# A two-layer hybrid trunk on one core: the LRU input joins the split products, and seven engine orders change

## What is computed

```python
h = rms_norm(x, norm_g)
proj = jnp.einsum('bsd,de->bse', h, w_in)
u_lru, u_s5, qkv_ret, q_nsa, kv_nsa, bg_nsa, gate_paths, merge = split_columns(proj, IN_SIZES)
...
ys = ys * jax.nn.silu(gate_paths.reshape(bsz, s, N_BRANCH, BRANCH_W))
branch = jnp.einsum('bsnw,nwd->bsnd', ys, w_branch)
merged = jnp.sum(jax.nn.sigmoid(merge.reshape(bsz, s, N_BRANCH, d)) * branch, axis=2)
return x + jnp.einsum('bsd,de->bse', merged, w_out)
```

## Time and profile before

| | |
|---|---|
| median of 3 runs | 856.46 us (855.59 to 857.69) |
| the profiled execution | 856.7 us, its span 854.9 us |
| TensorE matmuls busy | 796.3 us (93%) |
| VectorE, ScalarE, GpSimd busy | 517.6 (61%), 450.9 (53%), 305.2 us (36%) |
| mean granted TensorE clock | 0.961 |
| DMA | 126.6 MB, 148 GB/s over the span |

### The profile page before, as it was taken

How to read it: one execution, slowest core, us unless ns; L and a number is a source line. 1 busy time by engine, 2 the same in 40 slices (tenths; PEclk the granted TensorE clock), 3 DMA queues, 4 the chain that set the end, 5 groups by cost and what they waited for, 6 DMA issues and landing times.

```text
span 854.9 us, 11525 instructions
## 1 busy us (share of the span) xinstructions
PE 796.3 (93%) x4446; PEld 680.7 (80%) x4446; DVE 517.6 (61%) x761; ACT 450.9 (53%) x781; POOL 305.2 (36%) x135
## 2 busy tenths in 40 slices
PE   8786999899989899999989979998998989999996
PEld 8675889688978688887878868986897868888885
DVE  2957394477698551534686575547868875435335
ACT  5555786345752356553447297654474534545542
POOL 3000000005468576657400000000256775655860
PEclk9977999999998799999999989999999998999999
DMA  8518355466245434345435663535635344345541
GB/s 250 140 50 289 99 176 178 138 191 193 88 117 169 134 118 153 102 150 171 145 78 140 196 216 94 204 123 165 211 121 156 114 137 127 126 129 170 173 148 49
DMA packets 86998, 126.64 MB, mean 148 GB/s; under 512 B 22072, under 2 KB 32672, under 8 KB 86944
## 3 DMA queue, kind: packets, MB, share of 16 engines
q1 hardware_dynamic: 86768, 125.88, 47.5%
q10 hardware_dynamic: 176, 0.04, 0.0%
HBM read 124.85 MB, written 1.05 MB: 147 GB/s over the span
## 4 chain that ended last, share of the span: by engine, by line
PE 73%; ACT 9%; DVE 8%; issue 5%; POOL 2%; DMA 2%; ACTq 0%; POOLq 0%; DVEq 0%
PE proj L1662 52%; PE proj L1701 5%; PE M L1657 3%; ACT sc L698 2%; DMA raw<-in_w_in 2%; POOL w_lo L676 2%; PE M L1823 2%; ACT nkT L698 1%; ACT qT L698 1%; PE M L1976 1%; PE M L1981 1%; DVE sc L1539 1%; PE M L559 1%; ACT w_hi L698 1%; PE M L1824 1%
## 5 line engine op out<-in xcount | busy, mean ns | idle before, releaser
L676 POOL TENSOR_TENSOR w_lo<-raw,w_hi 128x1024 fp32r<-128x1024 f32 x112 | 287.1, 2596 | 501.2 <-ACT w_hi L698 469.9
L698 ACT ACTIVATE w_hi<-raw 128x1024 fp32r<-128x1024 f32 x192 | 197.4, 1055 | 125.0 <-DMA raw<-in_w_in 68.1
L1662 PE MATMUL proj<-w_hi,h_hi 128*128 128x512 f32 x544 | 220.5, 405 | 8.2 <-DVE w_lo L1247 7.7
L1662 PE MATMUL proj<-w_lo,h_hi 128*128 128x512 f32 x544 | 215.6, 396 | 0.0
L1662 PE MATMUL proj<-w_hi,h_lo 128*128 128x512 f32 x544 | 215.2, 396 | 0.0
L1662 PEld LDWEIGHTS proj<-w_hi,h_hi 128*128 128x128 f32 x544 | 104.3, 192 | 31.7 <-DVE w_lo L1247 8.5
L1662 PEld LDWEIGHTS proj<-w_hi,h_lo 128*128 128x128 f32 x544 | 104.2, 192 | 22.8
L1662 PEld LDWEIGHTS proj<-w_lo,h_hi 128*128 128x128 f32 x544 | 104.4, 192 | 21.0 <-issue 0.5
L1247 DVE TENSOR_TENSOR w_lo<-raw,w_hi 128x1024 fp32r<-128x1024 f32 x80 | 94.8, 1221 | 38.5 <-ACT w_hi L698 27.1
L1701 PE MATMUL proj<-h_full,raw 128*128 128x256 f32 x256 | 59.3, 393 | 7.8 <-ACT u_s L698 7.8
L1701 PEld LDWEIGHTS proj<-h_full,raw 128*128 128x128 f32 x256 | 50.1, 198 | 15.5 <-ACT u_s L698 8.3
(11 more groups left out here) (330 smaller groups left out, 1294.0 us busy)
## 6 DMA issues: line engine op xcount, KB each, us to landing
raw<-in_w_in SPq DMA_DIRECT2D x152, 512.0 KB, 3.7
raw<-in_w_branch SPq DMA_DIRECT2D x32, 512.0 KB, 3.6
raw<-in_w_out SPq DMA_DIRECT2D x16, 512.0 KB, 3.6
raw<-in_s_w_glu SPq DMA_DIRECT2D x8, 512.0 KB, 4.5
raw<-in_w_in SPq DMA_DIRECT2D x8, 256.0 KB, 2.6
merged<-in_nsa_ck_w SPq DMA_DIRECT2D x4, 512.0 KB, 5.2
mt<-in_nsa_ck_w SPq DMA_DIRECT2D x4, 512.0 KB, 6.8
merged<-in_nsa_cv_w SPq DMA_DIRECT2D x4, 512.0 KB, 4.6
```

Of the source, the lines that this page charges most:

```text
L676: nc.gpsimd.tensor_tensor(w_lo[:, slot(s, l), 0:n * w], raw[:, u % N_RAW, 0:n * w], w_hi[:, slot(s, l), 0:n * w].bitcast(f32), ALU.subtrac ...
L698: i = nc.scalar.activation(out_, in_, func, **kw)
L1662: last = mm(dst, left[i], right[j], start=start and n == 0, stop=stop and n == 2, skip_group_check=True)
```

## The change

u_lru leaves `NATIVE` and joins `LO_ON_VECTOR`: its four units are cast by ScalarE, their w_lo made by VectorE, and the chunk becomes a split product. Seven engine orders change with it:

1. ScalarE, start of a layer: the copy of u_s5 comes first, `keep_u` reads that copy, `keep_v0` stands before `trig(0)`, `spread_v(0)` behind the copies of cmp, and single casts stand between the copies up to ret_v. `spread_w(0)` now stands behind the wait for u_s5.
2. VectorE, start: `parameters_c` (cut off `parameters_b`) opens the layer; the h_lo stand before `make_w(1)`; the w_lo of u_lru stand around `make_v(0)` and `make_v(1)`. TensorE's wait for the h_lo moves ahead of u_lru.
3. SyncE: the loads of ck stand two units later.
4. ScalarE: the copies of nsa_kv no longer have casts ahead of them.
5. ScalarE: the tanh of the hidden layer stands ahead of `merge_chunk("s5", 0)`.
6. VectorE: the key rotation moves to before merge_s5_0, the query rotation to behind `rope_ret(1)`, reading PSUM with scaled tables; TensorE waits for its read before glu_b.
7. ScalarE: the exp of the compressed scores stands ahead of the copy that waits for `rnT_done`.

```diff
-NATIVE = ("u_s5", "cmp", "u_lru")
+NATIVE = ("u_s5", "cmp")
-LO_ON_VECTOR = ("ret_v", "nsa_kv", "gate_s5", ...
+LO_ON_VECTOR = ("u_lru", "ret_v", "nsa_kv", "gate_s5", ...
...
-                    cw1_at = {UNIT_END[CHUNK["u_lru"]] + 3: "ck", UNIT_END[CHUNK["gate_s5"]] + 2: "cv"}
+                    cw1_at = {UNIT_END[CHUNK["ret_v"]] + 1: "ck", UNIT_END[CHUNK["gate_s5"]] + 2: "cv"}
...
-                        src = pr("u_s5")[:, :].rearrange("p (q c j) -> p q c j", q=KB, j=LC)[:, :, :, LC - 1 - e]
+                        src = u_s5[:, :, :].rearrange("p q (c j) -> p q c j", j=LC)[:, :, :, LC - 1 - e]
...
+                    next_cast("u_s5")
+                    run(flat(u_s5[:, :, :]), pr("u_s5")[:, :], ACT.Copy, evac("u_s5"))
                     spread_w(0)
+                    keep_v0()
                     trig(0)
-                    keep_v0()
-                    next_cast("u_s5")
+                    cast_units(UNIT_END[CHUNK["cmp"]] + 2)
+                    act.wait_ge(evac("u_s5"), ev("u_s5"))
                     keep_u(0)
                     keep_u(1)
                     keep_wT(0, 0)
+                    cast_units(UNIT_END[CHUNK["cmp"]] + 3)
                     keep_u(2)
                     keep_u(3)
-                    run(flat(u_s5[:, :, :]), pr("u_s5")[:, :], ACT.Copy, evac("u_s5"))
                     keep_wT(0, 1)
-                    spread_v(0)
+                    cast_units(UNIT_END[CHUNK["cmp"]] + 4)
...
+                    spread_v(0)
                     cast_units(UNIT_END[CHUNK["u_lru"]] + 1)
...
-                    next_cast("u_lru")
+                    cast_units(UNIT_END[CHUNK["u_lru"]] + 2)
+                    act.wait_ge(chunk_done, ch("u_lru"))
                     run(u_lru[:, :, 3:T + 3], pr("u_lru")[:, :].rearrange("p (t n) -> p t n", t=KB), ACT.Copy, evac("u_lru"))
+                    cast_units(UNIT_END[CHUNK["u_lru"]] + 3)
+                    spread_w(1)
+                    cast_units(UNIT_END[CHUNK["ret_v"]])
+                    keep_wT(1, 0)
                     cast_units(UNIT_END[CHUNK["ret_v"]] + 1)
-                    spread_w(1)
                     keep_ms(0)
-                    keep_wT(1, 0)
...
-                    next_cast("nsa_kv")
+                    act.wait_ge(chunk_done, ch("nsa_kv"))
...
-                    merge_chunk("s5", 0)
                     act.wait_ge(hid_arg, 1)
                     run(hid_q, hid_q, ACT.Tanh, hid_tanh, scale=GELU_C)
+                    merge_chunk("s5", 0)
...
+                    act.wait_ge(cs_sub, 1)
+                    run(cols(3072, 256), cols(3072, 256), ACT.Exp, cs_exp)
                     act.wait_ge(rnT_done, 1)
                     run(flat(qT[:, :, :]), MF[:, 1024:2048], ACT.Copy, yr_ready)
-                    act.wait_ge(cs_sub, 1)
-                    run(cols(3072, 256), cols(3072, 256), ACT.Exp, cs_exp)
...
+                    parameters_c(l)
...
                     angles(0)
+                    for k in range(0, KD, 2):
+                        dve.wait_ge(hhi_done, k // 2 + 1)
+                        v.tensor_tensor(flat(h_lo[:, k:k + 2, :]), flat(h_full[:, k:k + 2, :]),
+                                        flat(h_hi[:, k:k + 2, :]).bitcast(f32), ALU.subtract).then_inc(hlo_done, 2)
                     make_w(1)
...
+                    def rotate(src, dst, at, read):
+                        shape = [P, TT, NHQ, 8]
...
+                        x1, x2_ = src[:, :, :, 0:8], src[:, :, :, 8:16]
+                        v.tensor_tensor(rope_n[:, 0], x1, cos, ALU.mult)
+                        v.tensor_tensor(rope_n[:, 1], x2_, sin, ALU.mult)
+                        v.tensor_tensor(rope_n[:, 2], x2_, cos, ALU.mult)
+                        v.tensor_tensor(rope_n[:, 3], x1, sin, ALU.mult).then_inc(read, 1)
+                        dve.wait_ge(read, 1)
+                        v.tensor_tensor(dst[:, :, :, 0:8], rope_n[:, 0], rope_n[:, 1], ALU.subtract)
+                        v.tensor_tensor(dst[:, :, :, 8:16], rope_n[:, 2], rope_n[:, 3], ALU.add).then_inc(nrope_ready, 1)
...
+                    split_lo("u_lru", 0, 1)
                     dve.wait_ge(v0_ready, 1)
                     make_v(0)
+                    split_lo("u_lru", 2)
                     make_v(1)
+                    split_lo("u_lru", 3)
...
                     skip(1)
+                    rotate(nk4, nk4, "", nk_read)
                     split_lo("merge_s5_0", 0)
...
-                    rope_nsa(rope_nsa_kd)
+                    dve.wait_ge(evac("nsa_q"), ev("nsa_q"))
                     dve.wait_ge(nrope_ready, 1)
+                    rotate(pr("nsa_q")[:, :].rearrange("p (a h c) -> p a h c", a=TT, h=NHQ), nq4, "_q", nq_read)
...
-                    dve.wait_ge(evac("nsa_q"), ev("nsa_q"))
-                    dve.wait_ge(yg_ready, 1)
-                    rope_nsa(nq4)
                     gate_times("ret")
...
-                                elif name in ("gate_s5", "gate_lru"):
+                                elif name in ("u_lru", "gate_s5", "gate_lru"):
...
+                    pe.wait_ge(hlo_done, KD)
                     chunk("u_lru", 0)
...
+                    pe.wait_ge(nq_read, 1)
                     chunk("glu_b")
```

More of the change, by code:

```diff
@@ L69 @@
 N_SPLIT = 5
-NATIVE = ("u_s5", "cmp", "u_lru")
+NATIVE = ("u_s5", "cmp")
 SPLIT_UNITS = [u for u in range(NU) if CHUNKS[UNITS[u][0]][0] not in NATIVE]
-LO_ON_VECTOR = ("ret_v", "nsa_kv", "gate_s5", "gate_lru", "merge_s5_0", "merge_s5_1", "ret_q", "ret_k", "nsa_q",
+LO_ON_VECTOR = ("u_lru", "ret_v", "nsa_kv", "gate_s5", "gate_lru", "merge_s5_0", "merge_s5_1", "ret_q", "ret_k", "nsa_q",
                 "out_0b", "out_1b")
@@ L160, in shape_constants @@
     put("nsa_cos", c), put("nsa_sin", s)
+    put("nsa_cos_q", c * f32(HD ** -0.5)), put("nsa_sin_q", s * f32(HD ** -0.5))
     c, s = rope((np.arange(32) % 16) * 16 + 31, 500000.0, HD // 4)
@@ L1092, in parameters_b, with parameters_c @@
                         link(v.tensor_tensor(S(17), S(19), S(16), ALU.subtract))
+                    def parameters_c(s):
+                        stage = Layer(vector, s)
                         stage.wait_ge(th_sin, 3)
@@ L1292, in branch @@
                             v.tensor_tensor(dst, dst, m, ALU.add).then_inc(mt_free, 1)
+                    nk4 = kd[:, :, :, :, :, :].rearrange("p a y h u d -> p a (y h u) d")
+                    def rotate(src, dst, at, read):
+                        shape = [P, TT, NHQ, 8]
+                        cos, sin = (bc(cst(f"nsa_{f}{at}").rearrange("p (a c) -> p a c", a=TT).unsqueeze(2), shape) for f in ("cos", "sin"))
+                        x1, x2_ = src[:, :, :, 0:8], src[:, :, :, 8:16]
[6 more added lines that the diff above has]
+                        v.tensor_tensor(dst[:, :, :, 8:16], rope_n[:, 2], rope_n[:, 3], ALU.add).then_inc(nrope_ready, 1)
                     def tap(k, t):
@@ L1309, in conv @@
                         i.then_inc(xc_ready, 1)
+                    split_lo("u_lru", 0, 1)
                     dve.wait_ge(v0_ready, 1)
                     make_v(0)
+                    split_lo("u_lru", 2)
                     make_v(1)
-                    for k in range(0, KD, 2):
-                        dve.wait_ge(hhi_done, k // 2 + 1)
-                        v.tensor_tensor(flat(h_lo[:, k:k + 2, :]), flat(h_full[:, k:k + 2, :]),
-                                        flat(h_hi[:, k:k + 2, :]).bitcast(f32), ALU.subtract).then_inc(hlo_done, 2)
+                    split_lo("u_lru", 3)
                     e, s_, s2, q_, m_ = S(1)[:, 0:4], S(6)[:, 0:4], S(6)[:, 4:8], S(7)[:, 0:4], S(7)[:, 4:8]
@@ L1420, in _ @@
                     rope_ret(1, "ret_k")
-                    def rope_nsa(x4):
-                        shape = [P, TT, NHQ, 8]
-                        cos = bc(cst("nsa_cos").rearrange("p (a c) -> p a c", a=TT).unsqueeze(2), shape)
-                        sin = bc(cst("nsa_sin").rearrange("p (a c) -> p a c", a=TT).unsqueeze(2), shape)
-                        x1, x2_ = x4[:, :, :, 0:8], x4[:, :, :, 8:16]
-                        v.tensor_tensor(rope_n[:, 0], x1, cos, ALU.mult)
-                        v.tensor_tensor(rope_n[:, 1], x2_, sin, ALU.mult)
-                        v.tensor_tensor(rope_n[:, 2], x2_, cos, ALU.mult)
-                        link(v.tensor_tensor(rope_n[:, 3], x1, sin, ALU.mult))
-                        v.tensor_tensor(x1, rope_n[:, 0], rope_n[:, 1], ALU.subtract)
-                        v.tensor_tensor(x2_, rope_n[:, 2], rope_n[:, 3], ALU.add).then_inc(nrope_ready, 1)
-                    rope_nsa_kd = kd[:, :, :, :, :, :].rearrange("p a y h u d -> p a (y h u) d")
-                    dve.wait_ge(evac("nsa_kv"), ev("nsa_kv"))
-                    dve.wait_ge(rope_ready, 2)
-                    rope_nsa(rope_nsa_kd)
+                    dve.wait_ge(evac("nsa_q"), ev("nsa_q"))
                     dve.wait_ge(nrope_ready, 1)
```

(3 more changed lines are left out.)

22 lines of the change are left out of this document (12 added, 10 removed).

## The result

The changed kernel takes 823.2 us (median of 4 runs, 820.26 to 827.89) where the kernel before, on the same chip, takes 856.03 us (854.24 to 857.69). The ratio is 0.9622, 95% interval 0.9571 to 0.9673: 32.8 us gained, where 47 were forecast. The profiled execution took 822.0 us with a span of 820.2 us and a mean granted clock of 0.972 (0.961 before).

What follows compares the result with a forecast made beforehand. TensorE, busy 796.3 of 854.9 us, was taken to bound the kernel, through its waits and the low clock after them. Terms of 10.8, 4.7, 11.1, 5.8 and 15.0 summed to 47.4 us, giving 809; range 799 to 829.

Steps and rivals of the forecast that it cites:

- the two starts: Starts of layers 1 and 2: reordered ScalarE and VectorE work shortens TensorE's waits; 10.8 and 0.5 us.
- merge_s5_0 after 140 in layer 1: Named sign that the prediction is wrong; merge_s5_0 was forecast to begin at 131.6 us, not 145.8.
- Hidden tanh: Around merge_s5_0: VectorE's 8.93 us wait for the tanh and TensorE's 3.8 us wait go; 11.1 us in all.
- exp: Compressed scores: the exp goes before a waiting copy, TensorE's 4.2 us wait goes; 15.0 us in all, clock included.
- rotations: Query rotation before glu_b, key rotation where GpSimd rests: TensorE's 2.05 us wait per layer goes; 5.8 us with clock.
- between the layers: Layer boundary: 23 small VectorE steps move, TensorE's wait falls from 3.7 to 1.1 us, matmuls reach full clock; 4.2 us.
- rival (b): Waits go, but the clock does not come back and new waits double their charge: 27.3 us, 829; chance 0.10.
- parts 2 and 3: Start of layer 1, net 10.8 us; between the layers with start of layer 2, net 4.7 us.
- The new wait before nsa_kv's second unit: Start of layer 1: its w_lo stands behind angles(1) on VectorE, so TensorE, there at 74.6, waits until 78.3.
- Rival (a): Starts give only the 2.6 us shorter wait between layers, as casts come too late: 34.5 us, 822; chance 0.20.
- The split product: u_lru's half chunks take 6.02 us instead of 7.07; TensorE saves 2.5 us per layer, as an upper end.
- rival (d): Starts: VectorE and ScalarE hand over to and fro, 32 w_lo waiting 1.9 us each, 61 us lost: 871; chance 0.03.

Runs made afterwards that it cites:

- e4: Kernel before with only the exp of the compressed scores moved ahead of the copy of the rotated retention blocks: 840.6 us, ratio 0.9815.
- e1: Changed kernel with keep_u reading a contiguous slice of u_s5 instead of every fourth element (S5 inputs differ from the reference's): 811.42 us, ratio 0.9469.
- e10: Changed kernel with u_s5 reordered in its copy out of PSUM, so keep_u reads 64 elements in a row and skip reads strided: 809.63 us, ratio 0.9454.
- e9: Changed kernel with keep_u out of PSUM and the copy behind it, spread_w(0) ahead of the u_s5 wait, trig(0) and casts later: 810.49 us, ratio 0.946.
- e2: Changed kernel with u_lru computed in one float32 pass again, without its split product and casts: 814.04 us, ratio 0.9511.
- e8: Changed kernel with only ScalarE's start order changed: spread_w(0) ahead of the wait for u_s5, trig(0) behind keep_wT(0, 1): 822.77 us, ratio 0.9602.
- e11: On top of e10: spread_w(0) before u_s5, keep_u ahead of casts, trig(0) late, nsa_kv's second low halves one place earlier: 796.9 us, ratio 0.931.
- e3: Kernel before with only the hidden tanh moved ahead of merge_chunk s5, 0 in ScalarE's program: 843.97 us, ratio 0.985.
- e7: Changed kernel with keep_u reading u_s5 from PSUM again, the copy behind it and some casts and keep_wT(0, 0) moved later: 812.38 us, ratio 0.948.

## Why the prediction was right or wrong

The direction, the range and the mechanism behind four of the six terms were right. The time forecast, 809, was 14 us too low, and the whole miss lies in the two starts. Of the other signs that were named, the mean clock came out as said (0.972), the sum of TensorE's waits did not (29.7 us, under 25 forecast), and by the prediction's own sign of being wrong (merge_s5_0 after 140 in layer 1) it was wrong, at 140.7.

1. **Hidden tanh, exp, rotations, between the layers**: 11.1, 15.0, 5.8 and 4.2 forecast; 11.5, 16.0, 5.5 and 4.3 in the trace of after; 12.0, 15.4, 5.9 and 3.6 alone. Each was read off one wait, its releaser and the next one in line, and the clock behind it was priced from the same matmuls at the other level. The first half of rival (b), a clock that does not come back, fell here: e4 gives 15.4 us for waits of 8.5. Its second half, new waits at double charge, is what happened at the starts (part 5). The key rotation's steps took 0.29 us where GpSimd rests, as forecast.

2. **The step that failed** is in parts 2 and 3: "ScalarE lets state_inputs(0) go at 47" (it was 51.9) and "10.6 + 5.0 + 3.2 = 18.8 us" (it was 23.9). The 10.6 held sixteen pieces at the 0.38 us that they took out of PSUM. The diff changed their source, and I carried the duration over as though it were the instruction's own. They took 0.66, which is 4.5 us a layer, and 0.41 without the stride (e1, e10). The rest is in the main a cast's wait of 0.5 us for its transfer.

3. **What followed from it.** In layer 2 the wait was 8.2 us and not 2.9, and the clock of 0.50 that came with it ran from 446.7 to 463.8, of which 11.7 us were work at half speed: 5.8 lost, where 1.7 was charged for each new wait. ret_v came 40.4 us behind the end of u_s5, not 29.7. In layer 1, 4.4 us of wait that I hadn't forecast and 9.1 us at half clock behind it; ret_v came at 67.07, not 58. VectorE's line was not unbroken either: from 30 to 85.4 it was busy 46.9 of 55.4 us, as forecast, but stood idle for 8.5 where 1.5 was allowed, 3.6 of them for ScalarE's w_hi. So nsa_kv's second unit began at 85.4 and not 78.3.

4. **The new wait before nsa_kv's second unit** came, with VectorE as its releaser: 2.6 us, 3.7 forecast.

5. **The price of a wait in clock was too flat.** I charged 1.7 us for each new wait. Measured: 1.7 behind waits of 2.2 and 2.6 us (3.4 us at the low level), 4.5 to 5.8 behind 4.4 and 8.2. The length of a wait alone does not give the price: e9's wait of 3.0 us in layer 1 had no low clock behind it for 29 us, e10's of 1.9 had 6.8 us of it, e2's of 3.9 had 13.7.

6. **Rival (a)** comes nearest to what happened at the starts: its time was 822, and 823.2 was measured. That the times agree so well is partly luck: it had the starts at 0 each, where they gave +5.2 and -7.7, and the other four terms came 2.8 us above its sum. It named the place, ScalarE's one line of 18.8 us, but as a matter of casts; e8 shows that casts and transfers hold it too once the other work is away, and e1 that the pieces do first. Its chance of 0.20 was too low, since both starts were sums over one long line of ScalarE, where any term that grows reaches TensorE in full. The forecast of 58 us for ret_v could be had (57.57 in e11), with short pieces and another order; strided pieces in that order were not tried.

7. **The split product** (2.5 us a layer as an upper end) was worth less than nothing here: e2 is faster without it. It takes time from TensorE where TensorE waits, and gives ScalarE three casts ahead of the last piece that it waits for. In e11, where that wait is gone, its half chunks of 6.0 us against 7.07 are time won; that e11 with a native u_lru would be slower was not tried.

Two slips in the prediction's sums change nothing: 8.5 and 6.8 for the compressed exp are 15.3, not 15.2, and rival (d) comes to 870, not 871.

What stays open: low clock for 3.4 or 6.8 us appears in some kernels near 251 to 263 and near 637 to 668, behind no wait over 0.8 us, and not in others (none near 251 to 263 in the changed kernel, 256.2 to 263.0 in e9). One stretch costs 1.7 or 3.4 us, which is much of the spread between runs of one kernel (e1: 806 to 817, at mean clocks of 0.985 and 0.972). What brings it was not settled. The same holds for 3.4 us at the low level near 10 to 15, which e1, e2, e3, e7 and e9 have and the changed kernel has not.

## What to carry to other kernels

When an edit changes where an instruction reads, its old duration is no row for the new one: look for a row with the same engine, source memory and stride, and if there is none, bound it. Before moving work out from in front of a transfer, ask what transfer it covered; and before making an engine's work shorter, ask whether it waits right behind it. A tensor that is read with a stride many times can be reordered once, in a copy that has to be made anyway: in e10 that took 3.9 us a layer off the pieces for 0.8 us more in skip.

## What the hardware showed that I had not expected

ScalarE, pieces of 32x256 float32: from PSUM with a stride of four elements 0.376 us, from SBUF in rows of 64 elements 0.414 to 0.415, from SBUF with a stride of four elements 0.658. A 128x1024 copy out of PSUM takes 1.02 us with that stride or without. VectorE's step on 128x256 rose from 0.48 to 0.67 us when its SBUF operands were read with strides (e10).

The Trainium skill, "SBUF — State Buffer", section "Door 1: The DMA port swizzle", says that SBUF is read in lines of 16 bytes, that full bandwidth needs two hits in a line, and that each step to a new line costs something. Four float32 are 16 bytes, so each element of the strided piece opens a line; e1 and e10 agree, with 0.24 us for 256 elements. The same place also names four float32 as how far one can stride for free; a stride of four was not free here, and the measurement decides. The prediction did not use this rule. The same page gives PSUM lines of 8 bytes and a cost for matmuls; ScalarE's reads of PSUM show no such cost here (the 128x1024 copy takes 1.02 us either way).
